# Down projection weights in 16 KB runs: four adjacent rows per partition, and one gate/up pass for 32-token blocks

## What is computed

```python
h = rmsnorm(x, g_pre_ffn) * (1 + sc2) + sh2            # 256 x 1024
logits = h @ w_router + b_router                       # 32 experts, top 4 of each token
gu = xblk @ w_gate_up[e] + b_gate_up[e]                # 1024 -> 2048, 8 MB of weights
x_glu = minimum(gu[:, :1024], 7)
x_lin = clip(gu[:, 1024:], -7, 7)
act = x_glu * sigmoid(1.702 * x_glu) * (x_lin + 1)
y = act @ w_down[e] + b_down[e]                        # 1024 -> 1024, 4 MB of weights
out = x + gt2 * rmsnorm(sum of gate * y, g_post_ffn)
```

## Time and profile before

| | |
|---|---|
| median of 3 runs | 1183.96 us (1181.68 to 1184.78) |
| the profiled execution's own time | 1179.82 us |
| its span, first to last instruction | 1177.6 us |
| TensorE busy | 1029.8 us (87%) |
| VectorE, ScalarE, GpSimd busy | 294.7, 179.7, 31.6 us |
| read from HBM | 462.50 MB, 395 GB/s over the span |

### The profile page before, as it was taken

How to read it: one execution, slowest core, us unless ns; L and a number is a source line. 1 busy time by engine, 2 the same in 40 slices (tenths; PEclk the granted TensorE clock), 3 DMA queues, 4 the chain that set the end, 5 groups by cost and what they waited for, 6 DMA issues and landing times.

```text
span 1177.6 us, 21864 instructions
## 1 busy us (share of the span) xinstructions
PE 1029.8 (87%) x8300; PEld 500.5 (43%) x8301; DVE 294.7 (25%) x813; ACT 179.7 (15%) x453; POOL 31.6 (3%) x54
## 2 busy tenths in 40 slices
PE   4999999977788999899979898989898989797965
PEld 3847887433342343334333433343334333333322
DVE  4636664242111221112111211121112111111112
ACT  3213340221111111101110111011101110101002
POOL 1001002210000000000000000000000000000000
PEclk9999999978899999999999999999999999798988
DMA  9899835989999999999999999999999999999994
GB/s 351 322 384 379 336 119 209 425 356 425 422 426 421 429 425 425 426 381 427 425 424 427 424 426 425 427 426 425 424 426 425 426 426 425 426 425 425 425 425 197
DMA packets 61484, 464.91 MB, mean 395 GB/s; under 512 B 5900, under 2 KB 10060, under 8 KB 28568
## 3 DMA queue, kind: packets, MB, share of 16 engines
q1 hardware_dynamic: 51808, 397.45, 81.7%
q10 hardware_dynamic: 9320, 66.11, 13.5%
q0 software_dynamic: 336, 1.07, 0.3%
HBM read 462.50 MB, written 2.11 MB: 395 GB/s over the span
## 4 chain that ended last, share of the span: by engine, by line
PE 58%; DMA 27%; DVE 4%; SPq 3%; issue 3%; ACT 2%; ACTq 1%; POOL 0%; DVEq 0%
PE pp L1537 21%; DMA arena<-in_w_down_dram 12%; PE pp L1568 11%; DMA bgu<-in_b_gate_up_dram 9%; PE pp L1323 5%; DMA arena<-in_w_gate_up_dram 4%; PE pp L1501 4%; PE pp L1245 3%; PE pp L1336 2%; PE pp L1255 2%; PE po L1398 2%; PE pp L1510 2%; PE po L1482 2%; SPq L374 1%; DMA arena<-in_w_ada_dram 1%
## 5 line engine op out<-in xcount | busy, mean ns | idle before, releaser
L1537 PE MATMUL pp<-arena,work 128*32 128x256 f32 (+1 forms) x3840 | 388.7, 461 | 42.9 <-ACT work L709 41.0
L1537 PEld LDWEIGHTS pp<-arena,work 128*32 128x32 f32 (+1 forms) x3840 | 167.1, 121 | 248.6 <-issue 142.0
L1568 PE MATMUL pp<-arena,work 128*32 128x256 f32 (+1 forms) x1920 | 194.5, 442 | 28.8 <-DMA arena<-in_w_down_dram 21.6
L1089 DVE TENSOR_SCALAR work<-pp 128x128 f32<-128x128 f32 (+1 forms) x74 | 24.9, 337 | 441.8 <-PE pp L1537 441.8
L1568 PEld LDWEIGHTS pp<-arena,work 128*32 128x32 f32 (+1 forms) x1920 | 77.2, 118 | 128.2 <-issue 82.4
L1501 PE MATMUL pp<-h_sb,work 128*32 128x256 f32 (+1 forms) x480 | 68.0, 490 | 37.7 <-DMA bgu<-in_b_gate_up_dram 18.1
L712 ACT ACTIVATE work<-work 128x128 f32<-128x128 f32 (+1 forms) x74 | 25.9, 350 | 419.3 <-DVE work L1089 419.3
L1482 PE MATMUL po<-work 64*128 64x512 f32 x304 | 75.5, 615 | 1.2 <-ACT work L728 1.2
L1083 DVE COPY work<-pp 128x256 f32<-128x256 f32 (+1 forms) x37 | 19.4, 525 | 211.4 <-PE pp L1501 211.4
L1323 PE MATMUL pp<-arena 128*128 128x256 f32 x256 | 57.1, 382 | 0.0
L1501 PEld LDWEIGHTS pp<-h_sb,work 128*32 128x32 f32 (+1 forms) x480 | 22.4, 125 | 79.3 <-issue 48.8
(11 more groups left out here) (224 smaller groups left out, 602.6 us busy)
## 6 DMA issues: line engine op xcount, KB each, us to landing
arena<-in_w_gate_up_dram SPq DMA_DIRECT2D x128, 2048.0 KB, 32.1
arena<-in_w_down_dram SPq DMA_DIRECT2D x32, 2048.0 KB, 36.2
arena<-in_w_down_dram ACTq DMA_DIRECT2D x62, 1024.0 KB, 13.8
arena<-in_w_ada_dram SPq DMA_DIRECT2D x11, 2048.0 KB, 14.1
arena<-in_w_in_dram SPq DMA_DIRECT2D x4, 2048.0 KB, 19.6
arena<-in_w_gate_dram SPq DMA_DIRECT2D x4, 2048.0 KB, 13.2
arena<-in_w_out_dram SPq DMA_DIRECT2D x2, 2048.0 KB, 10.3
arena<-in_w_ada_dram SPq DMA_DIRECT2D x2, 1024.0 KB, 13.2
```

The costliest lines, as they stand in the source:

```text
L1537: mm = t_.matmul(pp[j * m:(j + 1) * m, UP[hh], 0:w].rearrange("p (s f) -> p s f", s=2), hgT[:, at:at + m], gu_w[slot][:, k, :, r * PAIR:(r ...
L1568: mm = t_.matmul(pp[j * m:(j + 1) * m, UP[0], 0:w], actT[:, at:at + m], wd[:, j * w:(j + 1) * w], start=(n == 0), stop=(n == KD - 1))
```

## The change

- w_down is seen as groups of 512 rows, of which a partition holds four adjacent ones. So the lower half of down is one 2 MB transfer and the upper half another, both of one 16 KB run for each partition. `load_dhi` issues one transfer with one semaphore, `s_dhi`, and TensorE waits for it before the fifth down step (before: one wait before the fifth step, another before the seventh).
- Row order of down must agree with the activation's, so gate/up columns are now dealt in pairs: of every four columns, the first two go to one place and the next two to another (`pairs`). In wide blocks the two places are the banks `UP[0]` and `UP[1]`; the count and size of the matmuls stay.
- Narrow blocks no longer have two halves: all goes to `UP[0]`, with 512 columns for each matmul, and half as many of them. VectorE and ScalarE make one pass over 256 columns instead of two over 128 (`parts_of`), and semaphores step by 2.
- The buffer of the lower half of down is released after the fourth down step (`s_dlo_free`) instead of the sixth.
- BR, the run of a bias row, is 512 instead of 256: the bias of an expert comes as two rows instead of four, twice, in 2 KB pieces instead of 1 KB ones. `bgu` shares memory with the upper half of `gain2`, so that its first loads now wait for `s_gspill` (gain2 saved to HBM) and stand after the five first gate/up quarters. At the end, gain2 is read back into a page (`gain2_back`).

```diff
-BR = 256
+BR = 512
-        dn_v = w_down[0].rearrange("e (g p r) n -> e p g (r n)", p=P, r=2)
+        dn_v = w_down[0].rearrange("e (g p r) n -> e p g (r n)", p=P, r=4)
+        def parts_of(m, halves):
+
+            return (tuple(enumerate(halves)), 1) if m == TB else (((0, halves[1]),), 2)
-        def load_dhi(eng, e, r):
-            eng.dma_start(dhi_w[:, 2 * r:2 * r + 2, :].rearrange("p k d -> p (k d)"),
-                         dn_v[e, :, 2 + r, :]).then_inc(s_dhi[r], 16)
+        def load_dhi(eng, e):
+            eng.dma_start(dhi_w.rearrange("p k d -> p (k d)"), dn_v[e, :, 1, :]).then_inc(s_dhi, 16)
             def load_dlo(slot, e):
-                sp.dma_start(dlo_w[slot].rearrange("p (g r) d -> p g (r d)", r=2),
-                             dn_v[e, :, 0:2, :]).then_inc(s_dlo[slot], 16)
-
-            load_bgu(0, 0)
-            load_bgu(1, 1)
+                sp.dma_start(dlo_w[slot].rearrange("p k d -> p (k d)"),
+                             dn_v[e, :, 0, :]).then_inc(s_dlo[slot], 16)
...
+            sp.wait_ge(s_gspill, 16)
+            load_bgu(0, 0)
+            load_bgu(1, 1)
             sp.wait_ge(s_merged, KD)
...
-                    sp.wait_ge(s_dhi_free, total)
+                    sp.wait_ge(s_dlo_free, total)
...
-                def half_of(j, hh):
-                    return (2 * j + hh, slice(0, PAIR)) if w > PAIR else (j, slice(hh, PAIR, 2))
+                def columns_of(j, hh):
+                    return (j, hh) if m == TB else (j // 2, j % 2)
+
+                def up_of(j, hh):
+                    return pp[j * m:(j + 1) * m, UP[hh], :].rearrange("p (s n c) -> p s n c", s=2, c=2)
+
+                def pairs(cols, h):
+                    return cols.rearrange("p s (n h c) -> p s h n c", h=2, c=2)[:, :, h, :, :]
...
-                            r, cols = half_of(j, hh)
-                            mm = t_.matmul(pp[j * m:(j + 1) * m, UP[hh], 0:w].rearrange("p (s f) -> p s f", s=2),
-                                           hgT[:, at:at + m], gu_w[slot][:, k, :, r * PAIR:(r + 1) * PAIR][:, :, cols],
+                            g, h = columns_of(j, hh)
+                            mm = t_.matmul(up_of(j, hh), hgT[:, at:at + m],
+                                           pairs(gu_w[slot][:, k, :, g * BR:(g + 1) * BR], h),
...
-                    if k in (4, 6):
-                        pe.wait_ge(s_dhi[k // 2 - 2], dhi_landed)
-                    if n == 2:
+                    if n == 4:
+                        pe.wait_ge(s_dhi, dhi_landed)
+                    if n == 2 and m == TB:
                         pe.wait_ge(s_aTev, halves[1])
...
-                    if n == 5:
-                        mm.then_inc(s_dhi_free, 1)
+                    if n == 3:
+                        mm.then_inc(s_dlo_free, 1)
```

More of the change, by code:

```diff
@@ L144, in block_program @@
         x1_back = page(0, TT * D).rearrange("p (t d) -> p t d", t=TT)
+        gain2_back = page(2, D)
         y_out = page(1, TT * D).rearrange("p (t d) -> p t d", t=TT)
@@ L148, in block_program @@
         acc = h_sb
-        gain2 = sb("gain2", [P, D])
+        gain2_bias = sb("gain2_bias", [P, D + BR])
+        gain2 = gain2_bias[:, 0:D]
         ident = sb("ident", [P, P])
@@ L278, in block_program @@
         s_dlo = [sem(f"s_dlo{b}") for b in range(2)]
-        s_dhi = [sem(f"s_dhi{r}") for r in range(2)]
-        s_dhi_free = sem("s_dhi_free")
+        s_dhi = sem("s_dhi")
+        s_dlo_free = sem("s_dlo_free")
         s_nblk, s_selg = sem("s_nblk"), sem("s_selg")
@@ L437, in _ @@
             sp.wait_ge(s_lg, TT)
-            for r in range(2):
-                load_dhi(sp, 0, r)
+            load_dhi(sp, 0)
             sp.wait_ge(s_nblk, 1)
@@ L709, in block_of @@
                     a.copy(hgT[:, 0:w], pp[:, TURN, 0:w]).then_inc(s_turned, 1)
[L710 to L714, removed]
-                        act.wait_ge(s_aT, halves[hh])
-                        a.copy(actT[:, hh * w // 2:(hh + 1) * w // 2],
-                               pp[:, (TOKS, TURN)[hh], 0:w // 2]).then_inc(s_aTev, 1)
+                    parts, n_signals = parts_of(m, halves)
+                    for hh, n in parts:
+                        act.wait_ge(s_glu, n)
+                        a.activation(sig[:, hh, :], glu[:, hh, :], ACT.Sigmoid,
+                                     scale=ALPHA).then_inc(s_sig, n_signals)
+                    for hh, n in parts:
+                        act.wait_ge(s_aT, n)
+                        a.copy(actT[:, hh * PAIR:(hh + 1) * PAIR],
+                               pp[:, (TOKS, TURN)[hh], 0:PAIR]).then_inc(s_aTev, n_signals)
                     act.wait_ge(s_selT, it + 1)
@@ L744, in _ @@
                 act.wait_ge(s_y, item)
-                for r in range(2):
-                    load_dhi(act, e, r)
+                load_dhi(act, e)
                 place(n)
@@ L1506, in block_of @@
                 for j in range(tiles):
-                    for hh in range(2):
-                        rows = bias_rows_of(slot, hh)
-                        r, cols = half_of(j, hh)
-                        t_.matmul(pp[j * m:(j + 1) * m, UP[hh], 0:w].rearrange("p (s f) -> p s f", s=2),
-                                  pick[rows, r, 0:m], bgu[rows, :, cols], start=True, stop=False,
+                    for hh, _ in parts:
+                        g, h = columns_of(j, hh)
+                        rows = bias_rows_of(slot, h)
+                        t_.matmul(up_of(j, hh), pick[rows, g, 0:m], pairs(bgu[rows, :, :], h), start=True, stop=False,
                                   skip_group_check=True)
@@ L1518, in block_of, with turn_part @@
                 mm.then_inc(s_turn, 1)
-                def turn_half(hh):
-                    pe.wait_ge(s_actv, halves[hh])
-                    for i in range(q // 2):
-                        mm = t_.transpose(pp[:, (TOKS, TURN)[hh], i * P:(i + 1) * P], sig[:, hh, i:w // 2:q // 2],
-                                          ident[:])
-                    mm.then_inc(s_aT, 1)
+                def turn_part(hh, n):
+                    pe.wait_ge(s_actv, n)
+                    for i in range(2):
+                        mm = t_.transpose(pp[:, (TOKS, TURN)[hh], i * P:(i + 1) * P], sig[:, hh, i:PAIR:2], ident[:])
+                    mm.then_inc(s_aT, n_signals)
                 pe.wait_ge(s_turned, it)
```

43 lines of the change are left out of this document (22 added, 21 removed).

## The result

The changed kernel takes 1186.88 us in the median of 20 runs (1183.71 to 1194.29), the kernel before 1182.04 us in 20 runs beside them (1177.45 to 1187.34). The ratio is 1.0046, 95% interval 1.0033 to 1.0058: by the ratio 5.4 us slower, where 4.5 us faster was forecast. The profiled execution took 1184.71 us, its span 1182.5 us; the mean granted clock was 0.955 (0.954 before), so the clock isn't the difference.

What follows compares the result with a forecast made beforehand. The prediction took the saturated DMA stream (426 GB/s) as the bound, with TensorE mostly hidden. Terms: -5.0 (longer runs) + 0.5 (bias) + 0 = -4.5 us, so 1179.5 us from 1183.96; range 1175 to 1185.5 us.

Steps and rivals of the forecast that it cites:

- The transfers' term: Down-weight transfers: joining two 8 KB packets into 16 KB saves 10 ns, 5.0 us in all, bounds 4.0 and 6.4.
- rival 1: Stream not shorter: 10 ns no property of length, or bias-carrying engines land last and lose 4.9 us; about 1183.5 us, chance 0.28.
- the estimate of 1.8 us: Joining down packets: 3 of 259 cycles, 3.6 ns for each packet, gains 1.8 us in all, giving 1182.2 us.
- whatever shortens TensorE's blocks is hidden: TensorE's blocks: shortening them gains nothing, unless in the tail or where the stream ran dry; 9% to spare on average.
- rival 3: Pairs slow TensorE's gate/up, deciding from about 15%; at 30% 1218 us; sign: wide L1537 over 15 us; chance 0.06.
- rival 2: The dry stretch at 520 us goes too: up to 3.1 us more gain, 1176.4 us, chance 0.14.
- wide gate/up: 0: Wide blocks' gate/up matmuls: reading pairs with gaps instead of a closed run costs 0.
- narrow gate/up: 0.3 us less: Narrow blocks: pass 0.5 us shorter, turns take back 0.2; net 0.3 us each, 7 us of TensorE, all hidden but the last.
- bias: 0.5 us: Bias loads: two rows instead of four, same bytes; cost taken as 0.5 us, bounded by 0 and 4.9 us.
- The upper half: Upper half of down as one transfer: lands in 10 to 13 us, TensorE's 21.6 us wait mostly goes, worth 0.
- Rival 4: Upper half crowds out gate/up quarters, up to 5 us later; up to 2 us at the end, 1186 us; chance 0.04.

Runs made afterwards that it cites:

- long_runs_alone: Kernel before with only the down weights in 16 KB runs, one transfer for each half: 0.9964 of the kernel before, 4.3 us faster.
- bias_twice: Kernel before with each block's bias matmuls issued twice on TensorE: 1.0092 of the kernel before, 10.9 us slower.
- banks: Changed kernel with gate columns in one PSUM bank and linear ones in the other, wide and narrow blocks: 1.0007 of the kernel before.
- closed_wide: Changed kernel with wide blocks reading closed runs of 256 gate/up and bias columns instead of pairs: 1.0009 of the kernel before.
- two_engines: Kernel before with each four-row bias transfer issued as two of two rows, same bytes and packets: 1.0027 of the kernel before, 3.2 us.
- table_banks: Changed kernel with gate and linear in separate banks, narrow turn in the other bank, all experts' bias loaded once: 0.9901 of the kernel before, 1169.63 us.
- table_before: Kernel before with all experts' bias loaded once into a table, no bias transfers in the loop: 0.9973 of the kernel before.
- bias_load_twice: Kernel before with each bias transfer issued a second time into unused rows: 1.0066 of the kernel before, 7.8 us slower.
- The runs with the table: All experts' bias loaded once, no bias transfers in the loop: kernel before 0.9973, changed kernel 0.9953, with separate banks and turn 0.9901, of the kernel before.
- turn_bank: Changed kernel with a narrow block's activation turned in the other PSUM bank: 1.0054 of the kernel before.

## Why the prediction was wrong

**The transfers' term held.** -5.0 us was forecast, -4.3 us measured (long_runs_alone), by the mechanism named: 618 ns for 16 KB. The first half of rival 1, that the 10 ns are no property of the length, falls. So does the estimate of 1.8 us from the Trainium skill (DMA: Bandwidth & Descriptors, Why small descriptors are slow (HBM only)), if narrowly: the interval begins at 0.17%, 2.0 us. That the gain is all the runs' and none of it the single transfer's is argued from the 618 ns and from the rate in the stretch of rows 2 (428 GB/s in long_runs_alone, 426 before), not run.

**The step "whatever shortens TensorE's blocks is hidden", read backwards, is the one that failed.** From "TensorE has 9% to spare on average" I took lengthenings to be hidden as well, and let rival 3 decide only from about 15%. But experts of two blocks come in runs, and the dry stretch of rows 7, with TensorE busy for 9.54 of 10 us, was the sign that there TensorE already set the pace. bias_twice shows the price: 10.9 us for 23 us more of TensorE, with the stream running dry in that stretch and in three others. Weighing a 9% average against a stretch that I had quoted myself was the error; I used that stretch as a possible gain (rival 2) and not as a possible loss.

**The step "wide gate/up: 0".** I priced pairs by their neighbour, every second value, and called that free, because narrow down with closed runs had the same mean with waits inside. That reading stands, but only for matmuls of 256 columns: 128 of them take 7.51 us with every second value (rows 9) and 7.51 with pairs (banks), and 32 of narrow down with closed runs 1.94, which makes 7.8 for 128. The price shows in the form with 512 columns: 14.62 against 13.95 us wide, 7.41 against 7.07 narrow. The error was to carry the zero from one form to the other. For wide blocks the pairs cost 0.67 us each, 4.8%, and 14 x 0.67 = 9.4 us of TensorE, of which closed_wide shows 4.4 us in the time. That is far from the 15% of rival 3, and 14.62 us is also under the 15 us that the prediction named as its sign, so the loss came without the sign. The Trainium skill's rule that two accesses in a 16-byte line are enough for full rate (SBUF — State Buffer, Door 1: The DMA port swizzle) would leave the wide pass at 13.95 us; it took 14.62, and the measurement decides.

**The step "narrow gate/up: 0.3 us less".** Gate/up fell by 0.10 us and not by 0.5, the bias step rose by 0.41 (not in the sum at all), and turns and waits rose by 0.5 where 0.2 was worked out. A narrow block became some 0.8 us longer, 23 x 0.8 = 18 us in all. At bias_twice's price that would cost 8 to 9 us, yet in the time it is hardly visible, and no run explains why: banks, where pass and bias are those of before, reads 1.0007 beside closed_wide's 1.0009, and the turn's bank gives 0.1% at most (0.9996 against 1.0007, overlapping).

**The step "bias: 0.5 us".** The mechanism was named with the upper bound of 4.9 us, and I took the value near the lower end since two engines of sixteen "would have to be the slow ones". They seem to be, because they carry the bias each time: two_engines measured 3.2 us, of the 4.9 of the upper bound. So the second half of rival 1 (those engines land last) was the better term, though not all of its size.

**The upper half** lands in 14.0 us in the median, for 2 MB, and not in 10 to 13. TensorE's wait at that line went from 21.6 us to 4.2 as forecast, and was hidden: the wait for the bias grew from 18.2 us to 32.9. Rival 4 isn't needed: long_runs_alone has the single transfer and is faster.

**What adds up.** -0.36% (long runs) + 0.27% (bias on two engines) + 0.37% (pairs in wide blocks) = +0.28%, and 0.46% was measured. The 0.18% left is within the intervals; narrow blocks and the turn may hold it, and no run here proves that. Other sums close less well: without long runs the change costs 1.05%, of which bias and pairs are 0.64%, and table_banks gains 0.99% where long runs and table_before make 0.63%. So the causes are shown, but their sizes don't simply add. That the lagging engines are those of the bias is argued from their number at the stream's end and from two_engines and bias_load_twice (0.27 and 0.66%), at a clock like that of the kernel before. The runs with the table go the same way (-0.27, -0.93%), but with the clock raised. The profile's views don't name engines, so it wasn't read directly.

## What to carry to other kernels

A kernel whose page shows a flat transfer rate can still be set by TensorE in a few stretches; look for the dips in the rate before calling any lengthening of a block hidden. Here nearly half of it was paid in two cases (10.9 of 23 us, 4.4 of 9.4) and next to nothing in a third, so give such an edit a range and not a zero. Small transfers that recur beside a saturated stream can cost several times their share of the bytes; look at which engines still work when the stream ends, and try loading them once. When a run raises the granted clock as well, its gain isn't the price of what it took out. Price a new access pattern against closed runs in the same form of matmul, not against another pattern that is taken to be free.

## What the hardware showed that was not expected

- Matmul operands read from SBUF as pairs out of every four fp32 values: 14.62 us against 13.95 us for the same 64 matmuls of 512 columns, and 7.41 against 7.07 for narrow ones. With 256 columns (128 matmuls) pairs and every second value both take 7.51 us.
- Eight narrow bias matmuls of 512 columns into one bank take 1.06 to 1.10 us, sixteen of 256 columns into two banks 0.69 us, with the same number of columns in all (with 64 rows of bias instead of two, in table_banks, the sixteen take 1.13 us).
- 16 KB for each expert, 0.13% of its 12.6 MB, costs 0.66% when loaded a second time. Taking it out of the stream went with 0.27 and 0.93% less time and a granted clock of 0.967 and 0.973 instead of 0.951 (0.953 in the changed kernel).
- The clock fell to its lower level for a part of one window while TensorE was busy for 4.97 of 5 us (granted clock 0.66 in turn_bank; the wide block took 16.24 us and not 14.62).
